# PEER feed-forward, values-only stage: TensorE reads the kept gates from the big gate table, in an unrolled loop

## The reference

```
q = (xc @ wq).reshape(c, PEER_HEADS, 2, half)
sc = einsum('thid,ikd->thik', q, keys)
...
idx = take_along_axis(cand_i.reshape(c, PEER_HEADS, -1), best_pos, axis=-1)
gate = softmax(best_s, axis=-1)
ue = u[idx]
ve = v[idx]
act = gelu(einsum('td,thkd->thk', xc, ue))
return einsum('thk,thkd->td', gate * act, ve)
```

## Time and profile before

| what | value |
|---|---|
| median of 3 runs | 2891.49 us (2882.84 to 2892.65) |
| profiled execution, its own time | 2897.78 us |
| its span | 2896.1 us |
| PE, DVE, ACT, POOL busy | 93%, 66%, 32%, 13% of the span |
| mean granted clock of TensorE | 0.97 |
| V-only stage, layer 0 | about 1673 to 1900 us |
| V-only stage, layer 1 | about 2656 to 2878 us |

### The profile page before, as it was taken

The page is one execution under the profiler, slowest core; times in us unless marked ns, Lnnn a source line. Parts: engine busy times, 40 slices in busy tenths (PEclk is TensorE's granted clock), DMA queues, the critical chain, the costliest instruction groups (busy, mean ns, idle before and its releaser), DMA issues.

```text
span 2896.1 us, 46812 instructions
## 1 busy us (share of the span) xinstructions
PE 2679.6 (93%) x17212; PEld 2412.8 (83%) x17212; DVE 1904.4 (66%) x4138; ACT 929.1 (32%) x2023; POOL 368.6 (13%) x421
## 2 busy tenths in 40 slices
PE   8999999999999999998999878889999899998888
PEld 5888888778888788997999877868889889898886
DVE  6888888556665786789644455448857994444552
ACT  4222222334763665215311110035651261111011
POOL 0000000000000000017411122100000192112220
PEclk9999999999999999999999999999999999999999
DMA  7333333223313334595799999823336948999993
GB/s 300 115 115 112 120 125 123 76 89 117 117 44 117 117 118 155 182 377 190 263 377 387 377 386 379 326 99 111 123 131 237 388 172 330 392 384 387 367 406 142
DMA packets 90946, 642.45 MB, mean 222 GB/s; under 512 B 10096, under 2 KB 10480, under 8 KB 14256
## 3 DMA queue, kind: packets, MB, share of 16 engines
q1 hardware_dynamic: 60480, 420.23, 38.7%
q0 software_dynamic: 30320, 220.35, 19.2%
HBM read 639.49 MB, written 1.05 MB: 221 GB/s over the span
## 4 chain that ended last, share of the span: by engine, by line
PE 64%; DVE 14%; DMA 13%; issue 4%; ACT 2%; DVEq 2%; ACTq 0%; POOL 0%; POOLq 0%
DMA arena<-in_experts,arena 13%; PE bank L2518 12%; PE bank L489 10%; PE bank L491 9%; PE bank L490 9%; PE bank L2459 4%; PE bank L2510 4%; DVE arena L2563 2%; PE bank L1671 2%; DVE arena L2810 2%; DVE res L2568 2%; PE bank L2495 1%; PE bank L992 1%; PE bank L981 1%; PE bank L1365 1%
## 5 line engine op out<-in xcount | busy, mean ns | idle before, releaser
L2518 PE MATMUL bank<-arena,wring 128*128 128x160 f32 x4096 | 624.2, 313 | 112.2 <-DVE arena L2832 48.8
L2518 PEld LDWEIGHTS bank<-arena,wring 128*128 128x128 f32 x4096 | 600.1, 200 | 127.9 <-DVE arena L2836 53.9
L2576 POOL DMA_INDIRECT arena<-in_experts,arena x192 | 212.0, 1104 | 1806.3 <-DVE arena L2785 999.4
L473 DVE TENSOR_TENSOR peer_r<-wring,peer_r 128x512 fp32r<-128x512 f32 x440 | 296.4, 698 | 215.7 <-ACT peer_r L468 212.8
L489 PE MATMUL bank<-h_r,peer_r 128*128 128x512 f32 (+1 forms) x1088 | 397.4, 365 | 4.8 <-DVE h_r L503 3.4
L491 PE MATMUL bank<-h_r,peer_r 128*128 128x512 f32 (+1 forms) x1088 | 384.9, 354 | 0.0
L468 ACT ACTIVATE peer_r<-wring 128x512 fp32r<-128x512 f32 x440 | 266.7, 628 | 233.5 <-PE bank L491 228.6
L2563 DVE SCALAR_TENSOR_TENSOR arena<-arena,res 128x1024 f32<-128x1024 f32 x128 | 156.8, 1225 | 275.2 <-DMA arena<-in_experts,arena 273.9
L490 PE MATMUL bank<-h_r,peer_r 128*128 128x512 f32 (+1 forms) x960 | 334.2, 348 | 0.0
L2553 ACT ACTIVATE arena<-arena 128x1 f32<-128x1 f32 x192 | 38.8, 202 | 766.9 <-DVE arena L2563 766.8
L2459 PE MATMUL bank<-res,wring 128*128 128x160 f32 x1920 | 268.2, 303 | 12.8 <-ACT arena L2616 12.8
(11 more groups left out here) (411 smaller groups left out, 4101.2 us busy)
## 6 DMA issues: line engine op xcount, KB each, us to landing
wring<-in_w_peer SPq DMA_DIRECT2D x256, 1024.0 KB
wring<-in_w_proj SPq DMA_DIRECT2D x34, 1024.0 KB
wring<-in_w_hy SPq DMA_DIRECT2D x32, 1024.0 KB
arena<-in_w_ada POOLq DMA_DIRECT2D x16, 1024.0 KB, 5.1
wring<-in_w_out SPq DMA_DIRECT2D x16, 1024.0 KB
wring<-in_w_ada SPq DMA_DIRECT2D x8, 1024.0 KB
wring<-in_w_hyout SPq DMA_DIRECT2D x8, 1024.0 KB
wring<-in_w_q SPq DMA_DIRECT2D x8, 1024.0 KB
```

The source lines that it names most:

```text
L473: v.tensor_tensor(SPLIT[:, buf, 1, :], raw_quarter(name, i, j, q), SPLIT[:, buf, 0, :].bitcast(F32), ALU.subtract).then_inc(split_lo, 1)
L2518: mm = pe.matmul(expert_sum(k), w[:, k * P:(k + 1) * P], GP[:, par, :], start=False, stop=True, skip_group_check=True)
L2576: pool.indirect_dma_start(ROWS_IN[:, slot, :, :].rearrange("p a c -> p (a c)"), None, A[f"experts{l}"], bass.IndirectOffsetOnAxis(ap=GIDX[ ...
```

## The change

`rows_product` takes its gates from `GP` only in the MAIN loop. In the V-only stage it takes them from `G[:, n, :]` directly. For that the loop over the 76 blocks is written out, since n is then a constant. The 16 products `mid_kept` times gate are made in place in `G`, one after the other, right after the gate of the last MAIN block. The 60 copies are gone. `gp_ready` counts 68 per layer in place of 128; the EARLY products don't wait for it. The gather steps, POOL's loop, the weight stream and ACT's work are unchanged but for the counts.

```diff
             def rows_product(n, par, name, i, chunk, at):
 
                 w = wait_chunk(pe, name, i, chunk)[:, at:at + D]
-                pe.wait_ge(gp_ready, GP0 + BLOCKS * l + n + 3)
+                if name[:4] == "peer" or n < MAIN + MID:
+                    pe.wait_ge(gp_ready, GP0 + (MAIN + MID) * l + n + 3)
+                gates = GP[:, par, :] if name[:4] == "peer" else G[:, n, :]
                 for k in range(KT):
-                    mm = pe.matmul(expert_sum(k), w[:, k * P:(k + 1) * P], GP[:, par, :], start=False, stop=True,
+                    mm = pe.matmul(expert_sum(k), w[:, k * P:(k + 1) * P], gates, start=False, stop=True,
                                    skip_group_check=True)
                 mm.then_inc(v_used, 1)
...
-            full, rest = divmod(KEPT, 2 * RING)
-            with pe.Fori(0, full) as i:
-                for q in range(2 * RING):
-                    rows_product(MAIN + 2 * RING * i + q, q % 2, f"post{l}", i, q // 2, (q % 2) * D)
-            for q in range(rest - 1):
-                rows_product(MAIN + 2 * RING * full + q, q % 2, f"post{l}", full, q // 2, (q % 2) * D)
+            def late_product(q):
+                i, j = divmod(q // 2, RING)
+                rows_product(MAIN + q, q % 2, f"post{l}", i, j, (q % 2) * D)
+
+            for q in range(KEPT - 1):
+                late_product(q)
             pe.wait_ge(gathered, GATHERED0 + l + 1)
...
-            rows_product(BLOCKS - 1, 1, f"post{l}", full, (rest - 1) // 2, D)
+            late_product(KEPT - 1)
...
             def gate(n):
                 par = n % 2
-                src = G[:, n, :]
+                b, use = bank_of(name, n // RING, n % RING)
+                v.wait_ge(bank_free[b], use + 2)
+                v.wait_ge(v_used, BLOCKS * l + n + 1)
+                v.tensor_tensor(GP[:, par, :], GA[:, par, :], G[:, n, :], ALU.mult).then_inc(gp_ready, 1)
+
+            for n in range(BLOCKS):
                 if n < MAIN:
-                    b, use = bank_of(name, n // RING, n % RING)
-                    v.wait_ge(bank_free[b], use + 2)
-                v.wait_ge(v_used, BLOCKS * l + n + 1)
-                if n < MAIN:
-                    v.tensor_tensor(GP[:, par, :], GA[:, par, :], src, ALU.mult).then_inc(gp_ready, 1)
-                elif n < MAIN + MID:
-                    v.tensor_tensor(GP[:, par, :], mid_kept(n - MAIN, 1)[:, 0, :], src, ALU.mult).then_inc(gp_ready, 1)
-                else:
-                    v.tensor_copy(GP[:, par, :], src).then_inc(gp_ready, 1)
-
-            for n in range(BLOCKS):
-                gate(n)
+                    gate(n)
+                if n == MAIN - 1:
+                    for m in range(MAIN, MAIN + MID):
+                        v.tensor_tensor(G[:, m, :], mid_kept(m - MAIN, 1)[:, 0, :], G[:, m, :], ALU.mult).then_inc(gp_ready, 1)
                 if n in VALUES_AT:
                     gather_step(v, l, VALUES_AT[n])
```

More of the change, by code:

```diff
@@ L2669, in peer_scalar @@
                     act.wait_ge(u_done, U0 + MAIN * l + n + 1)
-                    act.wait_ge(gp_ready, GP0 + BLOCKS * l + n + 1)
+                    act.wait_ge(gp_ready, GP0 + (MAIN + MID) * l + n + 1)
                     act.activation(GA[:, n % 2, :], bank[b][:, 0:TD], ACT.Gelu).then_inc(bank_free[b], 1)
@@ L2704, in peer_pool @@
                 if n == MAIN + MID + 2 and l + 1 < DEPTH:
-                    pool.wait_ge(gp_ready, GP0 + BLOCKS * l + MAIN + MID + 2)
+                    pool.wait_ge(gp_ready, GP0 + (MAIN + MID) * (l + 1) + 2)
                     pool.dma_start(wide_t[:], A["wide"][l + 1]).then_inc(wide_again, 16)
```

## The result

The changed kernel takes 2859.08 us (median of 4 runs, 2857.7 to 2860.5). The kernel before takes 2887.96 us with one run more than stood above (4 runs, 2882.84 to 2892.65). The ratio is 0.9898 (95% interval 0.9881 to 0.9916), some 29 us. Run again beside the experiments, the ratio was 0.9894 (0.9872 to 0.9917). The profiled execution took 2859.69 us (span 2858.0), 38.1 less than the one of before.

The account below looks back on a forecast made before the run. It took TensorE, DVE and POOL waiting on each other in the V-only stage as the bound, with DMA near its end. Pace 26, less 6 for the 16 products, plus tail 22 gave 42 us saved: 2849.5 us, range 2827 to 2873.

Parts of the forecast that it names:

- the link: V-only stage: TensorE waits for DVE, DVE for gathered rows, POOL's issues for products; cutting this chain was to bring the gain.
- the work: DVE's 60 copies and 16 products between gather steps, 19 us a layer; removing this busy time was worth nothing.
- Pace: V-only gather steps fall to 4.71 us, by 0.30 in layer 1 and 0.43 in layer 0: 26 us saved.
- Tail: End of V-only stage: 6 products left after the gathers in place of 11; 10.9 us a layer, 22 saved.
- The 16 products: Made ahead of the V-only stage's first gather step, they delay it: 3 us a layer, 6 lost in sum.
- The unrolling: Writing out the V-only loop needs some 9.2 instruction packets a layer, priced at 0 us for TensorE.
- The clock: Mean granted clock of the V-only stage, 0.95 and 0.93, may come back a little; counted as nothing.
- Pace stays: Rival: the gathers' own round keeps V-only steps at 5.0 us and only the end saves time: 2870 us; chance 0.22.
- slower: Rival: instruction packets land late on queues full of gathers and weights: 2944 us; chance 0.04.
- The gathers get half: Rival: V-only gathers get half of 421 GB/s, 4.98 us each; no products left at their end: 2843 us; chance 0.10.

Follow-up runs that it names:

- the two half runs: Written-out loop without copies but with DVE's signal and wait kept: 1.0041 of before; changed kernel with the 60 copies kept, without any wait: 0.9886 of before.

## Why the prediction was right or wrong

**Direction, time and cause were right.** 2849.5 was forecast and 2859.1 came, in the range. I named the link as the cause and not the work, and the two half runs show it.

**Pace: right.** 0.30 and 0.43 us a step were forecast, and 0.28 and 0.37 came (4.73 and 4.77 against the 4.71 of the bytes), 23.4 us in place of 26. Its ground, that the bytes bound and not the gathers' round, held when half of the weights were left out.

**Tail: right in size, for another reason.** 10.9 us a layer were forecast, 10.4 and 10.8 came. I had said that 7 blocks would still have to land when the gathers are done. That held at 2808.5, when the last rows had landed (3.60 MB), but not at the last add, where 1.65 MB was missing: in between, the weights had both queues' rate to themselves. TensorE's last 9 products ran without a gap from 2807.80, so what set the tail was TensorE's own pace over the products that it still had to make, and not the landing of weights. That the size came out so well is luck in part.

**The 16 products: right where I looked, nothing over the stage.** 3 us a layer were forecast, and the first add starts 2.5 and 2.2 us later than before. But with them in the MAIN loop the stage gets no shorter, and both ratios stay: the delay is hidden behind the bytes. Against spreading them the run in front is worth 4 to 5 us a layer.

**The unrolling: the step failed in a part.** I took 0 us. Alone it costs 0.28% (8 us), with the link still there. With the link cut, TensorE waited 1.1 us for issue in the stage of layer 1, so nothing of that cost is to be seen. So this price does not simply add to the other terms. The count of packets was about right: 9.2 a layer forecast, 10 measured. The Trainium skill (Runtime: NRT & Kernel Launch, "Instruction fetch mechanics") ties the stall of a taken branch to a target that is not in the current pages, a condition that I had left out. The trace of before has 2 instruction packets in each layer's stage, for 9 turns of the loop, so the turns fetched nothing anew and there was no such stall to win back.

**The clock: counted as nothing, and not told apart.** It rose from 0.95 and 0.93 to 0.99, and a row of a V product now takes 0.143 us in place of 0.148 (161.96 us for 1132 rows, 152.96 for 1032). No run changes the clock alone. While bytes bound the stage, faster products only wait longer.

**The sum of the stage was right, and the sum of the kernel 10 to 13 us too large.** The two stages got 39.9 us shorter from trace to trace, against 42: 23.4 by pace and 21.2 by the tail, less 4.7 for the later first add. The profiled executions differ by 38.1, the medians by 28.9, and by 32.2 beside the later runs. The trace of before, from which all terms came, is of an execution above its median: 2897.78 us against 2887.96 here and 2892.91 to 2895.44 in three later sets of 17 runs, whose times go from 2876.53 to 2907.24. I took the full gain of that one execution off the median, and that is the step by which the sum was too large: the profiled execution of before is 9.8 us above its median here, that of the changed kernel 0.6. An estimate from one execution holds for that one; where the link costs 5.14 us a step in one layer and 5.01 in the next, it may cost less in the median execution. Whether the faster executions of the kernel before are shorter in these stages or elsewhere is not shown, as there is one trace of it. The two MAIN loops together took 518.8 us in it, and 520.6 and 520.0 in the two of the changed kernel, so none of the gain is there.

**The rivals.** "Pace stays" and "slower" are out. "The gathers get half" had the right mechanism: while both queues have work, each moves 1.05 MB in 4.97 us, for which I had worked out 4.98. The Trainium skill (DMA: Bandwidth & Descriptors, "Queues, rings and completion order") describes such a round robin, and the trace agrees. It had the wrong end, since POOL's order holds the weights back now and then, and the gathers catch up in a short step. Where that order was taken away, the short steps went and the kernel was 47.6 and 47.7 us faster than before (2847.8 and 2847.3), against the 48.8 of this rival.

## What to carry to other kernels

When an engine only hands data on that lies in memory already, ask what it stands behind, and not how long its copy takes: here 14 us a layer of copies cost nothing, and the place in DVE's queue behind a wait for a DMA cost 1%. Then look at who frees buffers: POOL, which waits for gathers, gave out the weights' slots as well, and letting the consumer free them was worth another half per cent. And a sum made from one execution of a loop of engines that wait for each other should be set against how much that kernel's own time varies.

## What was not expected of the hardware

A product whose first weight load carried the wait for DVE's copy started 0.29 us after the copy's start. Where the load carried the wait for the weights, and the wait for DVE was an instruction of its own ahead of it, it was 0.38.

Two busy DMA queues, gathers on one and weights on the other, moved 1.05 MB each in 4.97 us, and when the gathers had ended the weights alone moved at 419 GB/s.

The mean granted clock of the stage rose from 0.95 and 0.93 to 0.99 when TensorE's idle time in it fell from 31 and 33 us to 16.5 and 19. It was 1.00 in the run with half of the weights, where TensorE had no idle time, and also where TensorE frees the slots. There it still idles 10.8 of 179.6 us, nearly all of it in gaps of 0.35 us, one per pair of products:

```profile
2624.40:2804.00 179.60, 168.78 (x1187) 161.95 (x1187) 93.88 (x126) 18.01 (x73) 33.95 (x34) 1.00 0.99 408
```
